# Gaps between the tiles of the feed-forward's inner operand: what a row stride in SBUF does to a stream of fp32r matmuls

## The reference, cut to what matters

```python
h2 = rms_norm_2(x, norm2_w[l])
x = x + (jax.nn.silu(h2 @ w_ffn_gate[l]) * (h2 @ w_ffn_up[l])) @ w_ffn_down[l]
return rms_norm_2(x, norm_f_w)      # behind it, over the whole block's result
```

## Time and profile before

| what | value |
|---|---|
| median of 3 executions | 2247.58 us (2247.2 to 2247.77) |
| the profiled execution, span from first to last instruction | 2246.6 us |
| granted TensorE clock, mean | 0.999 |
| PE busy | 2226.5 us (99%), 11450 matmuls |
| PEld busy | 1838.2 us (82%) |
| VectorE busy | 1388.1 us (62%) |
| ScalarE busy | 1181.6 us (53%) |
| DMA | 426.77 MB, mean 190 GB/s |

### The profile page before, as it was taken

One profiled execution on the slowest core, in us unless ns is written; L12 is line 12 of the kernel. 1 busy time (PEld: TensorE's weight loads), 2 busy tenths in 40 slices (PEclk: granted clock), 3 DMA queues, 4 the chain that ended last, 5 costly groups with the idle time before them and its releaser, 6 DMA issues.

```text
span 2246.6 us, 28822 instructions
## 1 busy us (share of the span) xinstructions
PE 2226.5 (99%) x11450; PEld 1838.2 (82%) x11450; DVE 1388.1 (62%) x1860; ACT 1181.6 (53%) x1637; POOL 115.1 (5%) x101
## 2 busy tenths in 40 slices
PE   9999999999999999999999999999999999999998
PEld 7888888888888887888788888888888888888886
DVE  5677765757765677675665556765555455554555
ACT  5546665646665654554454555555444344534443
POOL 0003210002220121000000000000000000000000
PEclk9999999999999999999999999999999999999999
DMA  7456676656686764445644456667666566656663
GB/s 259 145 169 182 189 212 224 206 169 190 191 243 204 215 188 133 150 132 169 206 150 150 150 169 214 212 220 227 196 214 197 191 205 203 206 189 201 191 206 131
DMA packets 311302, 426.77 MB, mean 190 GB/s; under 512 B 118976, under 2 KB 119136, under 8 KB 311040
## 3 DMA queue, kind: packets, MB, share of 16 engines
q1 hardware_dynamic: 309008, 417.82, 58.9%
q0 software_dynamic: 1584, 6.16, 1.0%
q10 hardware_dynamic: 576, 0.95, 0.1%
HBM read 396.06 MB, written 2.10 MB: 177 GB/s over the span
## 4 chain that ended last, share of the span: by engine, by line
PE 95%; DVE 2%; ACT 1%; DMA 1%; issue 1%; POOL 0%; DVEq 0%; ACTq 0%
PE ACC L1004 29%; PE ACC L1006 28%; PE ACC L1005 28%; ACT arena L1033 1%; DVE WL L2104 1%; PE SCPV L597 1%; DMA W<-in_a_w_in 0%; PE TP L544 0%; ACT WH L1033 0%; PE SCPV L741 0%; PE SCPV L596 0%; PE SCPV L735 0%; PE SCPV L556 0%; PE SCPV L636 0%; PE SCPV L604 0%
## 5 line engine op out<-in xcount | busy, mean ns | idle before, releaser
L2104 DVE TENSOR_TENSOR WL<-W,WH 128x1024 fp32r<-128x1024 f32 x740 | 911.0, 1236 | 536.5 <-PE ACC L1006 360.1
L1004 PE MATMUL ACC<-WH,XH 128*128 128x512 f32 x2592 | 1040.0, 401 | 3.7 <-ACT arena L1033 2.3
L1006 PE MATMUL ACC<-WH,XL 128*128 128x512 f32 x2592 | 1011.1, 390 | 0.0
L1005 PE MATMUL ACC<-WL,XH 128*128 128x512 f32 x2592 | 1009.4, 389 | 0.0
L1033 ACT ACTIVATE WH<-W 128x1024 fp32r<-128x1024 f32 x740 | 757.0, 1051 | 322.5 <-PE ACC L1006 227.4
L1004 PEld LDWEIGHTS ACC<-WH,XH 128*128 128x128 f32 x2592 | 487.0, 188 | 112.2 <-issue 5.4
L1006 PEld LDWEIGHTS ACC<-WH,XL 128*128 128x128 f32 x2592 | 486.5, 188 | 104.2
L1005 PEld LDWEIGHTS ACC<-WL,XH 128*128 128x128 f32 x2592 | 487.4, 188 | 95.6 <-issue 1.2
L1004 PE MATMUL ACC<-WH,HH 128*128 128x512 f32 x328 | 128.8, 393 | 0.0
L1006 PE MATMUL ACC<-WH,HL 128*128 128x512 f32 x328 | 127.7, 389 | 0.0
L1005 PE MATMUL ACC<-WL,HH 128*128 128x512 f32 x328 | 127.7, 389 | 0.0
(11 more groups left out here) (308 smaller groups left out, 1368.2 us busy)
## 6 DMA issues: line engine op xcount, KB each, us to landing
W<-in_w_in SPq DMA_DIRECT2D x84, 1024.0 KB, 5.0
W<-in_a_w_in SPq DMA_DIRECT2D x47, 1024.0 KB, 5.3
W<-in_w_ffn_gate SPq DMA_DIRECT2D x44, 1024.0 KB, 5.2
W<-in_w_ffn_up SPq DMA_DIRECT2D x44, 1024.0 KB, 5.3
W<-in_w_ffn_down SPq DMA_DIRECT2D x44, 1024.0 KB, 5.1
W<-in_b_w_in SPq DMA_DIRECT2D x40, 1024.0 KB, 5.2
W<-in_a_w_out SPq DMA_DIRECT2D x16, 1024.0 KB, 5.9
W<-in_b_w_out SPq DMA_DIRECT2D x16, 1024.0 KB, 6.2
```

The costliest lines, as they stand in the source:

```text
L1004: MM(out, hx, WH[:, k, 0:ch.width], start=q == 0 and k == 0, stop=False)
L1005: MM(out, hx, WL[:, k, 0:ch.width], start=False, stop=False)
L1006: ins = MM(out, lx, WH[:, k, 0:ch.width], start=False, stop=last and k == QK - 1)
L2104: TT(tiles_of(M.WL[K.pair(n)], ch, half), tiles_of(M.W[n % 3], ch, half), tiles_of(M.WH[n % 3], ch, half).bitcast(F32), ALU.subtract).then ...
```

## The change

HH's 16 tiles of 256 elements get 16 unused elements (64 bytes) behind each, HL's get 4 (16 bytes), and the rows of `WL2` get 16 (64 bytes). `WL2` is allocated first now, and an unused tensor of 768 bytes follows, so that HH starts at 163968 and HL at 181376, again 128 more than a multiple of 1024. The instructions, their order and their waits are the same; two access patterns in `turn` are written with two dimensions, since two tiles of HH are no longer one run.

```diff
     SG, H = [sb(f"SG{i}", [P, TB, CH]) for i in range(2)], [sb(f"H{i}", [P, TB, CH]) for i in range(2)]
     M.SG, M.H = SG, H
-    HH, HL = sb("HH", [P, D // P, T], F32R), sb("HL", [P, D // P, T], F32R)
+    M.WL.append(sb("WL2", [P, QK, CH + 16], F32R)[:, :, 0:CH])
+    sb("operands_room", [P, 192])
+    HH, HL = (sb(name, [P, D // P, T + some], F32R)[:, :, 0:T] for name, some in (("HH", 16), ("HL", 4)))
     M.NF = sb("final_gain", [P, D])
-    M.WL.append(sb("WL2", [P, QK, CH], F32R))
     late = [sb(f"turning{i}", [P, 1024]) for i in range(3)]
...
             if gain is None:
-                A(hi[:, k:k + 2, :].rearrange("p k t -> p (k t)"), TP[j][:, :], ACT.Copy).then_inc(*did("turned_hi", key, 2 * c + j))
+                A(hi[:, k:k + 2, :], TP[j].rearrange("p (k t) -> p k t", k=2), ACT.Copy).then_inc(*did("turned_hi", key, 2 * c + j))
...
             if gain is None:
-                two = lambda x: x[:, k:k + 2, :].rearrange("p k t -> p (k t)")
-                TT(two(lo), TP[j][:, :], two(hi).bitcast(F32), ALU.subtract).then_inc(*did("turned", key, 2 * c + j))
+                TT(lo[:, k:k + 2, :], TP[j].rearrange("p (k t) -> p k t", k=2), hi[:, k:k + 2, :].bitcast(F32), ALU.subtract).then_inc(*did("turned", key, 2 * c + j))
```

## The result

The changed kernel takes 2252.99 us (median of 9 runs, 2251.98 to 2253.68) against 2247.27 us for the kernel before in the same comparison: a ratio of 1.0024, 95% interval 1.0015 to 1.0032. It is slower by 5.7 us, 0.24%. The time lies 0.01 us inside the predicted range of 2239.0 to 2253.0, and it is that of the rival that had 18%, not of the forecast of +0.6 us.

The account below looks back on a forecast made before the run. PE's matmul stream was taken to bound the kernel. The profiled 2246.6 us plus 0.6 for the HH and HL matmuls and 0 for the rest made 2247.2; timed runs lie 0.98 higher, giving 2248.2, range 2239.0 to 2253.0.

Parts of the forecast that it names:

- the price of a.kw: Chunk a.kw's rate per column, 115.8 ns per 256 columns, applied to 512: 231.6 against 226.8 ns, +5.1 us over 1056 matmuls.
- The bound: Whole kernel: PE, busy for 99% of 2246.6 us, sets the time; everything else counts only where PE waits.
- What can be gained, 14.3 us: Down chunks: 13.5 ns per matmul beyond streaming its columns, over 1056 matmuls, is all a better place could give.
- The faster rival: Down chunks: gaps part the two reads and cut the 13.5 ns excess; 2242.8 to 2233.3 us, chance 0.30.
- the term of the 704 + 352 matmuls: Matmuls with a tile of HH (704) or HL (352): a quarter of 2.5 ns, +0.6 ns each, +0.6 us.
- The 2.5 ns: Chunk a.kw: mean over best per matmul, 115.8 against 113.3 ns, read as the effect of where tiles begin.
- the slower rival: Down chunks: tiles beginning off the moving rows' place cost the stream more; +5.1 us, 2252.7 us, chance 0.18.
- The third rival: Down chunks: the 13.5 ns come from switching weights or a fixed load cost, whatever the address; 0 us, chance 0.27.
- The writes, the patterns, the order of the tensors: ScalarE and VectorE writes of HH and HL, two edited patterns in `turn`, new tensor order: each taken as 0.
- What would show it: Last chunk, first to last start: 16.1 us if unchanged, 15.3 or less if faster, 16.4 if slower; durations by line separate gaps.
- The sign of being wrong: The three down stretches together, 243.5 us, moving by more than 4.5 us.

Follow-up runs that it names:

- the sweeps: Matmul stream alone, no kernel: 72-matmul blocks with stationary tiles 0 to 512 bytes off the moving rows, upwards and downwards; 226.7 ns at 512, 233.3 at 64.
- the control: Changed kernel without gaps in HH, HL and `WL2`, keeping its tensor order and patterns, against the kernel before: 2246.65 against 2246.80 us, ratio 0.9997.
- the pairs: Matmul stream alone, 48-matmul blocks, high and low stationary tiles each at its own offset: 233.1 ns at (0, 32), 226.7 at (16, 16).

## Why the forecast was wrong on the size, point by point

That the time falls into the range is luck: the forecast was 2248.2 with an effect of +0.6 us, the effect is +5.7, and the range was wide because it had room for the rivals. Its upper end was set by the price of a.kw, which turned out near the truth for no good reason (see below).

**The bound.** Right: PE's stream of matmuls sets the time, only the 1056 matmuls over HH and HL moved, and the whole of their change shows in the time; PE is busy for the whole of all three down stretches after as before.

**What can be gained, 14.3 us.** The 13.5 ns over the columns exist, but no offset, pair or shift that I ran gave any of it back for this size. The faster rival, at 0.30, took the even distance of before for a handicap. It is the best of all places tried, and gaps break it.

**The step that failed** is the term of the 704 + 352 matmuls: "since a load of 128 columns passes over a whole 512 bytes, twice the 256 in which the places repeat, wherever it begins, I take a quarter of it: +0.6 ns". It measured +4.9 ns (5.22 us / 1056), eight times that. The period of 256 bytes was right, as the sweeps show. The averaging over it was not: a load at 64 bytes off passes over each place modulo 256 just as often and costs 6.6 ns more each time (233.3 against 226.7). Where it begins relative to the moving row decides, not what it passes over. The 2.5 ns that this quarter was taken of were mostly rounding: the trace has the tile at 59.39 us take 345 ns, 115.0 for each matmul and not 113.3, and the next tile, 64 bytes off, takes 345 as well; those 128 and 192 off take 350 and 353. So a.kw did not single out the moving rows' own place as the best.

**The upper bound and the slower rival.** +5.1 us, 2252.7, by the rate per column of a.kw, against +5.7 measured. The sign and the place were right. But its price was right by luck: at 128 loaded and 256 moving columns the offset of 64 is faster than 0 (117.8 against 119.7 ns), and at 64 loaded and 256 moving, nearest to a.kw's 80, the two are alike (113.3 and 113.5), so a.kw's 256-column matmuls could not stand for those of 512. A nearest row in another shape bounded the cost and explained nothing.

**The third rival**, no effect of addresses, is refuted by HH's and HL's 64-byte shift. The rule of the Trainium skill ("SBUF — State Buffer", section "Who interferes with whom") that PE has two independent read ports and never waits doesn't hold here to better than 3%: the distance of the two addresses alone, with no other engine at work, moves the stream from 226.7 to 233.3 ns. The Trainium skill's figure of 215.8 ns ("TensorE: Matmul & The Clock Gate", section "Back-to-back issue gap"), which that section gives for a matmul by itself, was reached by no block of 512 columns; the lowest is 226.65.

**The writes, the patterns, the order of the tensors: 0.** Right: 1060 and 685 ns as before, and the control at 0.9997. `WL2`'s padded rows were not tried alone; its 8 matmuls can hold 0.1 us.

**What would show it.** The 16.46 us of the last chunk are near the 16.4 named for the slower rival. The sign of being wrong came true: the three down stretches together were not to move by more than 4.5 us, and moved by 5.2. That the lines would tell HH's gaps from HL's did not come true, since one load out of step slows the matmuls of all three lines.

## What to carry to other kernels

Where TensorE streams 512 fp32r columns and loads 128 each time, let the stationary tiles and the moving rows begin alike modulo 256 bytes, and check it after every change to the allocation: 96 stray bytes cost this kernel 1.7%, and neither the page of the profile nor a wait names the cause. The sign to look for is the duration of a matmul: one value for all (389 ns) in step, a scatter of 387 to 398 or another even value (394) out of step. A block of 72 matmuls for each offset in one small program answers such a question better than any row of another shape.

## What the runs showed of the hardware that was not expected

- The distance modulo 256 bytes between what TensorE loads and what it streams sets the pace of 128x128 loads with 512 fp32r columns: 226.7 ns a matmul at 0, 256 and 512, around 233.3 at most other offsets, 228.9 at 192 (granted clock 1.00).
- A single load out of step in three costs far more than its third: 233.1 ns at 32 bytes and 231.4 at 64, where all three make 233.3.
- Near distance 0 it is ragged: 226.8 at 244 and 252 bytes, 233.2 at 248, 232.4 at 4, and 16 gave 233.3 in two sweeps and 226.7 in the pairs. What else decides there is open.
- Fewer loaded columns don't free the stream: 231.7 ns with 32 against 226.7 with 128 in step.
